# Who issues the gate/up weight loads, and which engine sums the down weight blocks, in a two-layer encoder

## The reference

```
for i in range(DEPTH):                      # DEPTH = 2
    h = rms_norm(x, norm_mix[i]);  x = x + mixer_i(h)
    h = rms_norm(x, norm_ffn[i]);  x = x + swiglu_ffn(h, w_gate_up[i], w_down[i])

def swiglu_ffn(h, w_gate_up, w_down):       # D_FF = 2816
    gu = einsum('btd,df->btf', h, w_gate_up);  g, u = gu[..., :D_FF], gu[..., D_FF:]
    return einsum('btf,fd->btd', silu(g) * u, w_down)
```

## Time and profile before

| | us |
|---|---|
| runs before, median of 3 | 1845.6 (1841.24 to 1848.66) |
| profiled execution | 1842.84 |
| its span | 1840.9 |
| PE busy | 1721.4 (94%) |
| DVE busy | 1234.8 (67%) |
| ACT busy | 754.5 (41%) |
| POOL busy | 344.5 (19%) |

### The profile page before, as it was taken

How to read it: one execution, slowest core, us unless ns; L and a number is a source line. 1 busy time by engine, 2 the same in 40 slices (tenths; PEclk the granted TensorE clock), 3 DMA queues, 4 the chain that set the end, 5 groups by cost and what they waited for, 6 DMA issues and landing times.

```text
span 1840.9 us, 20998 instructions
## 1 busy us (share of the span) xinstructions
PE 1721.4 (94%) x7741; PEld 1403.2 (76%) x7741; DVE 1234.8 (67%) x1572; ACT 754.5 (41%) x1149; POOL 344.5 (19%) x203
## 2 busy tenths in 40 slices
PE   6789999999999899889998999699999999998998
PEld 5568788788887788778776787478887878786887
DVE  5886555565658946765878877876556656579644
ACT  6444333333333335434576554343333333332332
POOL 2420000000008603223124213500000000049000
PEclk9889999999999999999999999899999999999999
DMA  4004323323376332243112112033342232482333
GB/s 168 23 19 134 106 92 108 93 92 113 93 256 207 92 97 81 69 120 109 47 52 63 35 47 80 23 103 103 92 127 91 92 114 86 156 312 75 105 97 119
DMA packets 185784, 188.39 MB, mean 102 GB/s; under 512 B 8354, under 2 KB 138452, under 8 KB 185684
## 3 DMA queue, kind: packets, MB, share of 16 engines
q1 hardware_dynamic: 185684, 187.07, 32.4%
HBM read 137.23 MB, written 44.56 MB: 99 GB/s over the span
## 4 chain that ended last, share of the span: by engine, by line
PE 32%; DVE 10%; ACT 3%; DMA 3%; issue 3%; POOL 0%; SPq 0%; DVEq 0%; ACTq 0%; POOLq 0%
PE bank L659 15%; PE bank L684 9%; PE bank L541 7%; DMA raw<-in_ffn_w_gate_up 2%; DVE a L1629 1%; DVE w L1625 1%; DVE raw_max L1909 1%; DVE ring L1556 1%; ACT pt_hi L1367 1%; PE bank L837 1%; DVE pt_lo L1963 0%; DVE f_t L1492 0%; ACT aw L920 0%; DMA raw<-act_d 0%; DVE raw L1611 0%
## 5 line engine op out<-in xcount | busy, mean ns | idle before, releaser
L659 PE MATMUL bank<-h_T,ring 128*128 128x512 f32 x2112 | 512.8, 395 | 32.1 <-DVE h_T L1503 11.9
L659 PEld LDWEIGHTS bank<-h_T,ring 128*128 128x128 f32 x2112 | 399.1, 190 | 128.7 <-ACT tmp L1043 18.6
L684 PE MATMUL bank<-a,w 128*128 128x512 f32 x1848 | 428.6, 393 | 16.5 <-DVE a L1629 13.6
L684 PEld LDWEIGHTS bank<-a,w 128*128 128x128 f32 x1848 | 348.7, 190 | 94.9 <-issue 22.7
L659 PE MATMUL bank<-h_B,ring 128*128 128x512 f32 x1584 | 387.8, 394 | 6.2 <-DVE h_B L1522 3.0
L659 PEld LDWEIGHTS bank<-h_B,ring 128*128 128x128 f32 x1584 | 299.7, 190 | 74.2 <-DVE h_B L1522 3.7
L1011 ACT CAST ring<-raw 128x512 fp32r<-128x512 f32 (+1 forms) x178 | 128.1, 720 | 191.7 <-DVE raw L1612 133.6
L2122 POOL TENSOR_TENSOR wd_A<-wd_A,wd_A 128x1024 f32<-128x1024 f32 (+1 forms) x12 | 35.4, 2947 | 873.6 <-DMA wd_A<-in_ffn_w_down 873.6
L1556 DVE TENSOR_TENSOR ring<-raw,ring 128x512 fp32r<-128x512 f32 (+1 forms) x178 | 147.8, 832 | 48.3 <-ACT ring L1011 48.3
L1625 DVE TENSOR_TENSOR w<-wd_A,w 128x1024 fp32r<-128x1024 f32 x72 | 98.1, 1363 | 110.9 <-ACT w L1085 110.9
L1629 DVE TENSOR_TENSOR a<-raw,a 128x1024 fp32r<-128x1024 f32 x84 | 140.9, 1678 | 10.9 <-ACT a L1087 10.9
(11 more groups left out here) (168 smaller groups left out, 2207.6 us busy)
## 6 DMA issues: line engine op xcount, KB each, us to landing
raw<-in_ffn_w_gate_up SPq DMA_DIRECT2D x88, 512.0 KB, 5.0
act_d<-tmp SPq DMA_DIRECT2D x154, 256.0 KB, 2.1
raw<-act_d SPq DMA_DIRECT2D x70, 512.0 KB, 3.7
wd_A<-in_ffn_w_down SPq DMA_DIRECT2D x40, 512.0 KB, 8.2
raw<-in_attn_w_qkv SPq DMA_DIRECT2D x24, 512.0 KB, 3.9
raw<-in_attn_w_o SPq DMA_DIRECT2D x16, 512.0 KB, 4.2
tmp<-tmp SPq DMA_DIRECT2D x80, 64.0 KB, 2.0
raw<-act_d SPq DMA_DIRECT2D x14, 256.0 KB, 2.7
```

What stands on the lines that cost most here:

```text
L659: ins = pe.matmul(out[:, :], w, m, start=k in (1, 2, 5) and j == 0 and t == 0, stop=k in (2, 3, 4) and j == 3 and t == 2, skip_group_check ...
L684: ins = pe.matmul(banks[m][:, :], w, h, start=q in (0, 1, 3) and first and t == 0, stop=q in (1, 5, 6) and jj == NBLK - 1 and t == 2, skip ...
```

## The change

Four things change; the sizes, the matmuls and the buffers stay.

1. From chunk 4 "gate" and chunk 5 "up" on, the weight loads are issued by ACT: the gate unit of chunk i+1 behind silu_0(i-1), the up unit of chunk i+2 behind the cast of A11(i+1). The waits of a load are the same ones, now on ACT.
2. SP keeps the stores. The first store of a chunk (B11 or B21, `store_act1`) is its own step and stands ahead of the others. In the first chunks load (3, 1) comes before store T1 of chunk 0, and load (4, 0) behind the stores of chunk 1.
3. The 24 sums of down weight blocks are made by DVE, one after the low parts of each of blocks 3 to 26, in place of POOL. Their order is: the twelve of A11 and s2 in turn, then six of A21, then six of A12; ACT's waits on `s2_sum` are renumbered to it.
4. The list `later` puts two A12 loads in front of each of the first three pairs A21, A22.

```diff
+        def load_gu(q, layer, i, gate):     # body as before, q in place of sp
+            ...
+            def store_act1(layer, i):
+                sp.wait_ge(act1, NF * layer + i + 1)
+                store(layer, i // 2, "B21" if i % 2 else "B11", act_tiles(layer, i)[1])
             def load_ffn(layer):
...
-                load_gu(layer, 3, 0)
-                store_even(layer, 0)
-                load_gu(layer, 3, 1)
-                store_odd(layer, 1)
+                load_gu(sp, layer, 3, 0)
+                store_act1(layer, 0)
+                load_gu(sp, layer, 3, 1)
+                store_even(layer, 0)
+                store_act1(layer, 1)
+                store_odd(layer, 1)
+                load_gu(sp, layer, 4, 0)
                 for i in range(3, NF):
-                    if i + 1 < NF:
-                        load_gu(layer, i + 1, 0)
+                    if i > 2:
+                        store_act1(layer, i - 1)
                     if (i - 1) % 2 == 0:
                         store_even(layer, i - 1)
                     else:
                         store_odd(layer, i - 1)
-                    if i + 1 < NF:
-                        load_gu(layer, i + 1, 1)
...
-                later = [("A12", jj) for jj in range(NBLK)]
+                later = []
                 for jj in range(NBLK):
+                    if jj < 3:
+                        later += [("A12", 2 * jj), ("A12", 2 * jj + 1)]
                     later += [("A21", jj), ("A22", jj)]
...
@@ ACT, swiglu
                     if i > 2:
                         silu_0(layer, i - 1)
+                        if i + 1 < NF:
+                            load_gu(act, layer, i + 1, 1)
                         w_split(layer, i, G_A22)
                         snap_p1(layer, i)
                         if i + 1 < NF:
                             w_split(layer, i + 1, G_A11)
+                        if i + 2 < NF:
+                            load_gu(act, layer, i + 2, 0)
@@ DVE
+            def down_sum(layer, n):
+                ...
+                if n < 12 and n % 2 == 0:
+                    dve.wait_ge(w2_lo, N_BLOCK * layer + jj + 1)
+                    dve.wait_ge(wd_in["A21"][jj // 2], 32 * (layer + 1))
+                    nc.vector.tensor_tensor(wd["A11"][:, part, :], wd["A11"][:, part, :], wd["A21"][:, part, :],
+                                            ALU.subtract).then_inc(s2_sum, 1)
+                ...
                 for k in range(2, 38):
                     block_lo(layer, k)
+                    if 3 <= k < 27:
+                        down_sum(layer, k - 3)
                     if k > 6 and k % 6 == 1:
                         add_rows(layer, k // 6 - 1)
@@ POOL, swiglu: the two loops that made the 24 sums are gone
```

More of the change, by code:

```diff
@@ L298, in y_copied, with gate_col @@
             eng.wait_ge(y_dve if u % 2 else y_act, u // 2 + 1)
+        def load_gu(q, layer, i, gate):
+            n = unit(layer, i, gate)
+            if layer == 0 and n < 2:
+                q.wait_ge(pw_lo_done, n + 1)
+            elif layer == 1 and i < 2 and (i, gate) != (1, 1):
+                q.wait_ge(w_lo, N_ATT)
+            elif n >= RAW:
+                prev = n - RAW - 2 * NF * layer
+                c = prev // 2
+                q.wait_ge(f_sum, 4 * (NF * layer + c + 1))
+                if prev % 2:
+                    q.wait_ge(f_lo, split_no(layer, c, G_A22))
+                else:
+                    q.wait_ge(f_lo, max(split_no(layer, c, G_S3), split_no(layer, c, G_A12)))
+            col = gate_col(gate) + i * P
+            q.dma_start(raw[:, n % RAW, :].rearrange("p (k f) -> p k f", k=KC),
+                         gu_rows[layer][:, :, col:col + P]).then_inc(fr_in[n % RAW], 16)
+        def gate_col(gate):
+            return 0 if gate else DFF
         @block.sync
@@ L355, in store_even @@
                 tiles = act_tiles(layer, i)
-                sp.wait_ge(act1, NF * layer + i + 1)
-                store(layer, j, "B11", tiles[1])
                 sp.wait_ge(t_1, NPAIR * layer + j + 1)
@@ L362, in store_odd @@
                 j = i // 2
-                sp.wait_ge(act1, NF * layer + i + 1)
-                store(layer, j, "B21", act_y[1])
                 sp.wait_ge(act0, NF * layer + i + 1)
@@ L409, in load_ffn @@
             def load_ffn(layer):
[L410 to L415, removed]
-                load_gu(layer, 3, 0)
+                load_gu(sp, layer, 0, 0)
+                load_gu(sp, layer, 0, 1)
+                load_gu(sp, layer, 1, 0)
+                load_gu(sp, layer, 1, 1)
+                load_gu(sp, layer, 2, 0)
+                load_gu(sp, layer, 2, 1)
+                load_gu(sp, layer, 3, 0)
+                store_act1(layer, 0)
+                load_gu(sp, layer, 3, 1)
                 store_even(layer, 0)
-                load_gu(layer, 3, 1)
+                store_act1(layer, 1)
                 store_odd(layer, 1)
+                load_gu(sp, layer, 4, 0)
                 for i in range(3, NF):
-                    if i + 1 < NF:
-                        load_gu(layer, i + 1, 0)
+                    if i > 2:
+                        store_act1(layer, i - 1)
                     if (i - 1) % 2 == 0:
@@ L434, in load_ffn @@
                     load_wd(layer, "A11", jj)
+                store_act1(layer, NF - 1)
                 store_odd(layer, NF - 1)
-                later = [("A12", jj) for jj in range(NBLK)]
+                later = []
                 for jj in range(NBLK):
+                    if jj < 3:
+                        later += [("A12", 2 * jj), ("A12", 2 * jj + 1)]
                     later += [("A21", jj), ("A22", jj)]
@@ L1076, in block_hi @@
                 elif q == 3:
-                    act.wait_ge(s2_sum, 24 * layer + 12 + 2 * jj + 1)
+                    act.wait_ge(s2_sum, 24 * layer + 12 + jj + 1)
                     src = wd["A21"][:, blk(k), :]
@@ L1082, in block_hi @@
                 else:
-                    act.wait_ge(s2_sum, 24 * layer + 12 + 2 * jj + 2)
+                    act.wait_ge(s2_sum, 24 * layer + 18 + jj + 1)
                     src = wd["A12"][:, blk(k), :]
@@ L1630, in block_lo @@
                                         a2[:, s, 0:n, 0, :].bitcast(F32), ALU.subtract).then_inc(a2_lo, 1)
+            def down_sum(layer, n):
+                done = 24 * layer
+                if n < 12:
+                    jj = n // 2
+                else:
+                    jj = (n - 12) % 6
+                part = blk(jj)
+                if n < 12 and n % 2 == 0:
[3 more added lines that the diff above has]
+                                            ALU.subtract).then_inc(s2_sum, 1)
+                elif n < 12:
+                    dve.wait_ge(wd_in["A22"][jj // 2], 32 * (layer + 1))
+                    dve.wait_ge(s2_sum, done + 2 * jj + 1)
+                    if jj == 2:
+                        for name in D_ACT:
+                            dve.wait_ge(stored[name], 16 * NPAIR * (layer + 1))
+                    nc.vector.tensor_tensor(s2_of(jj), wd["A22"][:, part, :], wd["A11"][:, part, :], ALU.subtract
+                                            ).then_inc(s2_sum, 1)
+                elif n < 18:
+                    nc.vector.tensor_tensor(wd["A21"][:, part, :], wd["A21"][:, part, :], wd["A22"][:, part, :],
+                                            ALU.add).then_inc(s2_sum, 1)
+                else:
+                    dve.wait_ge(w2_lo, N_BLOCK * layer + NBLK + jj + 1)
+                    dve.wait_ge(s2_sum, done + 2 * jj + 2)
+                    nc.vector.tensor_tensor(wd["A12"][:, part, :], wd["A12"][:, part, :], s2_of(jj), ALU.subtract
+                                            ).then_inc(s2_sum, 1)
             def add_rows(layer, q):
@@ L2116, in swiglu @@
                     t3_full(layer, j)
[L2118 to L2138, removed]
             for r in range(8):
```

## The result

| | before | after |
|---|---|---|
| runs, median (range) | 1843.4 us (1840.7 to 1848.7) | 1824.4 us (1822.2 to 1826.4) |
| profiled execution | 1842.84 | 1823.22 |
| span | 1840.9 | 1821.4 |
| granted clock, mean | 0.979 | 0.976 |

Ratio after to before 0.9893, 95% interval 0.9865 to 0.9921: 15 to 25 us faster. One execution of e1 took 2316.6 us at a granted clock of 0.70 and is left out; all others that are counted ran at 0.975 to 0.986.

What follows compares the result with a forecast made beforehand. TensorE, busy 1721.4 of 1840.9 us, was taken as the bound, so only removed PE stalls gain. -16.9 - 22.4 + 3.8 + 11.6 = -23.9 us gave 1818.9 for a profiled execution, 1822 as median; range 1806 to 1839.

Steps and rivals of the forecast that it cites:

- Loads on ACT: Gate/up stage: earlier loads issued by ACT remove all PE stalls before product 7, both layers together, -16.9 us.
- The limit: Gate/up chunks: DVE's first block sum must start by about 7.9 us into the chunk for no PE stall, 0.3 left.
- the rival drawn from it: Gate/up: loads land no earlier since they run beside the stores; 1839 us, no change by the bound; chance 0.08.
- ACT's issue: Gate/up: 0.57 us per load issue, hidden, cost 0; rival: far longer than on SP, 1865 at 4.7 us, chance 0.05.
- Chunk 2: Gate/up start: snap_p5 waits for a store now behind load (3,1); product 3 about 1.9 us later per layer, +3.8 us.
- the upper bound: Chunk 2 of gate/up: 2 x 3.5 us if the clock falls too.
- POOL's sums on DVE: Down stage: with POOL idle DVE's operations return to 1.22 us and the stalls go, -22.4 us.
- The price of a sum: Down stage: one 128x1024 sum on DVE takes 1.2 us, taken from the nearest rows, 1.23 and 3.42 with POOL.
- DVE's wait for A21 1: Down stage, first sum behind block 3: PE stalls 3.9 us plus 1.9 for the clock, 5.8 a layer, +11.6 us.
- The second gate: Down stage, sum behind block 7 waiting for A21 3: load lands at 569.6, DVE there at 567.6; no charge.
- vanished: Rival, down stage: weights land in time or PE's lead covers the wait, which costs nothing; 1810 us; chance 0.15.
- came three times: Rival, down stage: wait three times a layer, once per pair of A21 and A22 blocks, +23.2, 1845 us; chance 0.11.

Runs made afterwards that it cites:

- e1: Changed kernel with POOL's sums, the old weight list and the old s2_sum counts put back, so only the loads move to ACT; 1833.4 us, ratio 0.9929.
- e5: The changed kernel itself run again, unedited, in a second comparison; 1823.2 us, ratio 0.9869 to the kernel before.
- e7: Changed kernel, but SP issues all loads, gate and up load right behind the first store of chunk i-1; 1824.0 us, ratio 0.988.
- e9: Changed kernel, but ACT issues the gate load behind the cast of A11, just ahead of the up load; 1829.5 us, ratio 0.9915.
- e10: Changed kernel, but ACT issues both loads behind snap_p5, 5.7 us into the chunk; 1879.9 us in one run.
- e3: Changed kernel with store T1 of chunk 0 again ahead of load (3, 1); 1817.7 us, ratio 0.9844 to the kernel before.
- e4: Changed kernel with the down weights listed in pairs that share a semaphore; 1813.7 us, ratio 0.9821 to the kernel before.
- e8: Changed kernel with each sum two blocks later, behind blocks 5 to 28, weight list as changed; 1811.9 us, ratio 0.9815.

## Why the prediction was right, and where its sizes were off

The forecast was 1822 and the measured median 1824.4; in its own terms, one profiled execution, 1818.9 against 1823.2. The mechanism held in each part. That 1822 and 1824.4 lie so near owes a little to luck: the forecast stands on a median before of 1845.6, which with one more execution became 1843.4; the gain was forecast at 23.6 us and came out at 19.0, and at 23.9 in e5.

1. Loads on ACT: -16.9 forecast; the stretch of 133 products shrank by 10.1 and 6.8, 16.9. e1 shows that it comes from this part; e7 that the place in the order made it, not the issuer; e9 and e10 that DVE's wait costs PE nothing until a limit, and about its full length beyond it. The limit was worked out as 7.9 us into the chunk with 0.3 to spare and is about 8.3. The chunks that gained are the even ones, which the prediction calls odd; the sum took all of them from the stretch as a whole, so it is not touched. The rule of the Trainium skill that I weighed ("DMA: Bandwidth & Descriptors", "Issuing engines are not separate DMA queues") stands: e7 agrees with it, since one issuer gives 1824.0 us and two 1823.2 on the same chip. It was only the rival drawn from it, that the loads would land no earlier, that fell: they were late in SP's order, which the rule does not speak of.
2. ACT's issue: 0.57 us forecast, hidden; it takes 0.37 on the queue and starts at 256.40, while silu_0 runs from 256.34, and the next cast starts 0.54 after silu_0 where it was 0.49 in the kernel before. The engine lost 0.05 us there, not an issue's length.
3. Chunk 2: +3.8 forecast, +4.4 measured (1.4 in layer 0, 3.0 in layer 1). The stall was right: product 3 comes 1.8 and 1.9 us later than before, 1.9 forecast. The lower clock behind it, which the sum left to the upper bound, came in one layer of the two, and in e5, e7 and e1 in both. e3 takes the term away.
4. POOL's sums on DVE: -22.4 forecast. The stretch from block 8 to block 16 fell by 11.0 in layer 0, and e4's down stages are 11.1 and 11.4 below the kernel before: 22.5. The price of a sum, 1.23 us, was taken as 1.2.
5. DVE's wait for A21 1: +11.6 forecast, +14.7 measured, the term of the sum that was mis-sized. Of 1.6 us more in layer 0, 0.9 are the stall: block 4 starts 4.8 us late by the pace of 5.44 a block (3.9 forecast), since the load took 10.4 us to land where the slot had shown 8.9. The rest is the clock, 2.6 us in block 4 instead of the 1.9 of the earlier trace rows. The second gate cost nothing, as forecast: DVE waited 1.2 us there in layer 0 and 2.3 in layer 1, and PE not at all. e4 removes it by the order of the list, e8 by PE's lead; both gain the same 14.7.

The sum of the measured terms is -16.9 + 4.4 - 22.5 + 14.7 = -20.3; the rest of the program, which the change does not touch, was 1.1 us longer in this execution, and the span shows -19.5 (the last 0.3 is the cut at the stages' ends). Of the rivals, none held: the wait neither vanished nor came three times, the loads landed earlier, and ACT's issue took 0.37 us, no more than one of SP's (0.38).

## What to carry to other kernels

Put a load in the order of an engine at the point where its buffer comes free, ahead of stores whose data come later; which engine issues it made no difference that these runs can tell (e7). When work moves to an engine whose results PE needs each few microseconds, every wait moves with it, so check that what it waits for has landed: here the move itself was worth 22 us, and two badly placed transfers, one a layer, took two thirds of it back. Two transfers under one semaphore should stand next to each other in the list.

## What the runs showed of the hardware that I had not expected

- An issue on ACT's queue (0.37 us) runs beside ACT's own operation; the next one starts only 0.05 us later than without it.
- The clock behind stalls of PE of nearly the same length differs: after 2.14 us of idle 12 matmuls took 3.03 us, after 2.20 us 4.61 (granted clock 0.63). Before block 4, after 4.24 to 4.88 us of idle, it fell in all 14 stalls of the seven traces that have them: 24 matmuls took 6.9 to 8.3 us instead of 5.44, at a granted clock of 0.56 to 0.79.
- A load's time to land depends on the stretch: the gate load of 512 KB, issued 0.26 us into a chunk, took 3.5 to 4.8 us in the changed kernel, and 4.8 to 6.3 in the even chunks of e9, issued 3.06 us in. Loads of the same size at the start of the down stage took up to 11.2.
- DVE's additions that read a bank took 2.47 us for four both beside POOL's work and without it, while its subtractions with two operands in SBUF went from 1.22 to 3.42.
